# A two-layer decoder trunk on one core: the first layer reordered, and the dense feed-forward fed before its row norm is known

## What is computed

```python
x = x + concat([s5_mixer(u), memory_attention(q, mem)]) @ l0_w_out
h = rms_norm(x, ffn_norm)                      # y = x * rsqrt(mean(x*x) + eps) * g
x = x + (silu(h @ w_gate) * (h @ w_up)) @ w_down
...
kv = shared_kv(x);  x = x + concat([moba_attention(..), memory_attention(..)]) @ l1_w_out
h = rms_norm(x, l1_ffn_norm)
x = x + moe_swiglu(h, router, w_gate, w_up, w_down)     # top 2 of 8 experts
```

## Time and profile before

| | us |
|---|---|
| three runs | 1522.99, 1524.78, 1525.23 (median 1524.78) |
| the profiled execution | 1524.49 |
| its span | 1522.8 |
| PE busy | 1471.9 (97%) |
| DVE busy | 1190.7 (78%) |
| ACT busy | 973.8 (64%) |
| experts start (first expert matmul) | 520.2 |

### The profile page before, as it was taken

One profiled execution on the slowest core, in us unless ns is written; L12 is line 12 of the kernel. 1 busy time (PEld: TensorE's weight loads), 2 busy tenths in 40 slices (PEclk: granted clock), 3 DMA queues, 4 the chain that ended last, 5 costly groups with the idle time before them and its releaser, 6 DMA issues.

```text
span 1522.8 us, 20929 instructions
## 1 busy us (share of the span) xinstructions
PE 1471.9 (97%) x7935; PEld 1237.2 (81%) x7935; DVE 1190.7 (78%) x1211; ACT 973.8 (64%) x947; POOL 128.2 (8%) x151
## 2 busy tenths in 40 slices
PE   7999999999978999999999999999999999999997
PEld 3788789999756988888888888888888888888886
DVE  6883545455684798898898889889889889888987
ACT  4324354444451777777787787787777778778775
POOL 1751300000544000000000000000000000000000
PEclk9999999999999999999999999999999999999998
DMA  8434655344342499999999999999999999999992
GB/s 240 124 48 178 237 201 180 139 139 138 111 166 98 178 356 366 342 358 365 371 332 365 371 335 356 375 338 357 364 341 359 365 371 330 366 372 334 355 376 92
DMA packets 193090, 425.97 MB, mean 280 GB/s; under 512 B 14002, under 2 KB 23088, under 8 KB 192944
## 3 DMA queue, kind: packets, MB, share of 16 engines
q1 hardware_dynamic: 192736, 425.23, 78.2%
q10 hardware_dynamic: 304, 0.06, 0.0%
HBM read 421.67 MB, written 1.05 MB: 278 GB/s over the span
## 4 chain that ended last, share of the span: by engine, by line
PE 89%; DVE 5%; ACT 4%; issue 1%; POOL 1%; ACTq 0%; DVEq 0%
PE bank L413 75%; PE bank L513 3%; PE bank L433 2%; PE bank L466 2%; PE bank L849 2%; PE bank L861 1%; DVE w_lo L1733 1%; ACT work L1321 1%; PE bank L656 1%; DVE work L1726 1%; PE bank L567 1%; ACT work L1203 1%; DVE w_lo L1886 0%; PE bank L549 0%; PE bank L680 0%
## 5 line engine op out<-in xcount | busy, mean ns | idle before, releaser
L1886 DVE TENSOR_TENSOR w_lo<-ring,w_hi 128x2048 fp32r<-128x2048 f32 x342 | 779.9, 2289 | 104.6 <-ACT w_hi L1469 104.0
L1469 ACT ACTIVATE w_hi<-ring 128x2048 fp32r<-128x2048 f32 x342 | 651.9, 1918 | 125.5 <-PE bank L413 124.6
L413 PE MATMUL bank<-w_hi,xg_hl 128*128 128x512 f32 x1792 | 557.1, 392 | 0.2 <-issue 0.2
L413 PEld LDWEIGHTS bank<-w_hi,xg_hl 128*128 128x128 f32 x1792 | 332.8, 188 | 67.5 <-issue 0.4
L413 PE MATMUL bank<-w_lo,xg_hl 128*128 128x512 f32 x896 | 349.4, 390 | 0.0
L413 PE MATMUL bank<-w_hi,at_hl 128*128 128x512 f32 x896 | 277.5, 391 | 0.0
L413 PEld LDWEIGHTS bank<-w_lo,xg_hl 128*128 128x128 f32 x896 | 168.2, 188 | 35.8
L413 PEld LDWEIGHTS bank<-w_hi,at_hl 128*128 128x128 f32 x896 | 167.0, 188 | 34.0
L413 PE MATMUL bank<-w_lo,at_hl 128*128 128x512 f32 x448 | 174.5, 389 | 0.0
L1783 DVE TENSOR_TENSOR fpart_hl<-ring,fpart_hl 128x1024 fp32r<-128x1024 f32 x66 | 80.7, 1225 | 90.8 <-ACT fpart_hl L1384 90.4
L1384 ACT ACTIVATE fpart_hl<-ring 128x1024 fp32r<-128x1024 f32 x66 | 69.7, 1059 | 98.2 <-PE bank L413 98.2
(11 more groups left out here) (235 smaller groups left out, 1213.4 us busy)
## 6 DMA issues: line engine op xcount, KB each, us to landing
ring<-in_l_moe_w_gate SPq DMA_DIRECT2D x58, 2048.0 KB, 7.8
ring<-in_l_moe_w_up SPq DMA_DIRECT2D x57, 2048.0 KB, 7.8
ring<-in_l_moe_w_down SPq DMA_DIRECT2D x56, 2048.0 KB, 7.8
ring<-in_l_ffn_w_gate SPq DMA_DIRECT2D x5, 2048.0 KB, 8.8
ring<-in_l_ffn_w_up SPq DMA_DIRECT2D x5, 2048.0 KB, 8.9
ring<-in_l_ffn_w_down SPq DMA_DIRECT2D x5, 2048.0 KB, 7.7
ring<-in_l_w_in SPq DMA_DIRECT2D x4, 2048.0 KB, 8.4
ring<-in_l_w_out SPq DMA_DIRECT2D x4, 2048.0 KB, 8.1
```

The lines of the kernel that those rows point to most:

```text
L413: last = mm(p, lhsT=xs[a], rhs=ws[b], start=start and q == 0, stop=stop and q == 2, **kw)
L1469: ac(w_hi(n), at(e_slot(q) * SLOT + j * HALF, HALF), ACT.Copy).then_inc(S("hi"), 1)
L1886: tt(LO[e_slot(q)][:, j * HALF:(j + 1) * HALF], at(e_slot(q) * SLOT + j * HALF, HALF), w_hi(n).bitcast(fp), ALU.subtract).then_inc(S("lo"), 1)
```

## The change

The tensor block has most of it; line numbers of the new kernel are some 4 to 50 higher.

- First layer. `idle_products(5, 12)` stands ahead of `win0a`. The coefficient transposes are no longer together between the two halves of `win0b` but 16 ahead of k = 0 and 16 ahead of k = 5 of the second half. The three `Ug` flips are spread among the twelve `Bm` flips, `V` waits for each pair of `Bm` blocks when it comes to them rather than for all twelve, and `memkv1` no longer waits for the copies of `q0T` and `mkT`.
- wout0. The low halves get a buffer of their own (`CTL0`). `wide` takes both row halves m in one loop over k for `wout0a`; `wout0b` runs m = 0, then the flips of the first four column blocks of XS, then m = 1.
- Dense feed-forward. XS is flipped without the norm's row scale (`rows_f0` is gone, and the two `idle_products` with it). The last four blocks are flipped ahead of part 1. ACT squares after the flips are read. The scale comes back in two places: DVE makes two diagonal matrices `DG`, PE multiplies them by ones (`rsb`, ahead of part 4), DVE copies that to `RSB` and multiplies every gate block by it (`gate`) before the Silu; the residual of the down product is scaled by row (`scalar_tensor_tensor`).
- kv: the last down part finishes both row halves of columns 0 to 511 first, the flips follow block by block, `proj_kv` waits for each pair of blocks, and ACT squares after its first two blocks.
- wout1 and router: `wout1a` with both halves in one loop, flips after `wout1b`'s first half and at its end, router inputs in their own buffer `HTF`, idle products of 3, 5 and 8 calls where 6, 7 and 25 were.

```diff
+            idle_products(5, 12)
             proj_half("win0a", HT, "win0", 0, (0, 1, 2, 3), "xT0")
...
-            proj_half("win0b", HT, "win0", 1, (0, 1, 2, 3), None, coefficients)
+            proj_half("win0b", HT, "win0", 1, (0, 1, 2, 3), None, {0: (6, cm, "cm"), 5: (7, pw, "pw")})
...
-            for n in range(12):
-                read_out(pe, ("Bm", n))
             for n in range(3):
                 read_out(pe, ("Ug", n))
             vb = [unit(pe, ("V", n), n) for n in range(3)]
             for j in range(PAIRS):
+                if j % 4 == 0:
+                    for ri in range(2):
+                        read_out(pe, ("Bm", 6 * ri + j // 4))
...
-            for h, name in enumerate(("wout0a", "wout0b")):
-                for m in range(TM):
-                    wide(name, "wout0", h, m, 2 * h + m, (CTH0, HTHL[:, 1]), "wout0", state_space_and_memory)
+            def flip_cols(tag, q, b, parts):
+
+                p = unit(pe, ("T" + tag, q), b)
                 for m in range(TM):
+                    read_out(pe, parts[m])
+                    for k in (2 * q, 2 * q + 1):
+                        last = transpose(p[:, (k % 2) * T + m * P:(k % 2) * T + (m + 1) * P], XS[:, m, k * P:(k + 1) * P])
+                ready(last, ("T" + tag, q))
+
+            wide("wout0a", "wout0", 0, (0, 1), (0, 1), (CTH0, CTL0), "wout0", state_space_and_memory)
             mem_keys(1, (6, 7))
+            wide("wout0b", "wout0", 1, (0,), (4,), (CTH0, CTL0), "wout0")
+            for q in range(2):
+                flip_cols("f0", q, 6 + q, [("wout0", 0, m) for m in range(TM)])
+            wide("wout0b", "wout0", 1, (1,), (5,), (CTH0, CTL0), "wout0")
...
-            idle_products(5, 24)
-            rows_to_cols("f0")
-            idle_products(5, 7)
-            for q in range(4):
-                read_out(pe, ("Tf0", q))
...
+                if n == 1:
+                    for q in range(2, 4):
+                        flip_cols("f0", q, 4 + q, [("wout0", 1, m) for m in range(TM)])
+                if n == 4:
+                    pe.wait_ge(S("ones_f"), 1)
+                    pe.wait_ge(S("dg"), 1)
+                    p = unit(pe, "rsb", 6)
+                    for m in range(TM):
+                        last = mm(p[:, m * P:(m + 1) * P], lhsT=ONESF, rhs=DG[:, m], start=(m == 0), stop=True, skip_group_check=True)
+                    ready(last, "rsb")
...
-            rows_to_cols("kv", XS, [("ffn", b) for b in range(4)])
-            pe.wait_ge(S("ct_kv_act"), 2)
-            pe.wait_ge(S("ct_kv_dve"), 2)
-            proj_kv("kv", CT, "kv", (4, 5))
+            for q in range(4):
+                flip_cols("kv", q, q, [("ffn", q // 2 * 2 + m) for m in range(TM)])
+            proj_kv("kv", CT, "kv", (4, 5), lambda k: pe.wait_ge(S("ct_kv_act" if k < 4 else "ct_kv_dve"), k % 4 // 2 + 1))
...
+            idle_products(2, 5)
             pe.wait_ge(S("ld_router"), 16)
...
-            idle_products(7, 25)
+            idle_products(2, 8)
             pe.wait_ge(S("sel"), 1)
...
@@ scalar
-            norm("f0", 0, [("wout0", h, m) for h in range(2) for m in range(TM)])
+            mem_keys_out(1)
             for q in range(4):
                 p = got(act, ("Tf0", q))
...
+            for h in range(2):
+                for m in range(TM):
+                    read_out(act, ("wout0", h, m))
+            for m in range(TM):
+                ac(JUNK0[:, m], XS[:, m], ACT.Square, accum_out=ss[:, m:m + 1]).then_inc(S("ss_f0"), 1)
...
@@ vector
+                if n == NFP + 1:
+                    dve.wait_ge(S("rs_f0"), 1)
+                    for m in range(TM):
+                        last = tsc(DG[:, m], ident, rs[:, m:m + 1], None, ALU.mult)
+                    last.then_inc(S("dg"), 1)
...
+                    def gate(f):
+                        p = got(dve, ("h", c, f))
+                        tt(SG0[:, f], p[:, 0:T], RSB, ALU.mult).then_inc(S("gs"), 1)
+
+                    gate(0)
                     for f in range(FCH[c] // P):
+                        if f + 1 < FCH[c] // P:
+                            gate(f + 1)
                         n_sg += 1
                         dve.wait_ge(S("sg0"), n_sg)
                         free(tt(HID0[:, f], SG0[:, f], PS[units[("h", c, f)][0]][:, T:2 * T], ALU.mult), ("h", c, f))
```

191 lines of the change are left out of this document (107 added, 84 removed).

## The result

The changed kernel took 1513.19 us in the median (1512.1 to 1514.56, 4 runs) against 1525.01 for the kernel before (1522.99 to 1525.34, 4 runs): a ratio of 0.9929, 95% interval 0.9917 to 0.9942. The forecast was 1509.3, with a range of 1502.5 to 1515.0; faster was right, and 11.8 us were gained of the 15.2 forecast. The profiled execution took 1513.77, its span is 1512.0.

A forecast was written before the change was run, and what follows sets the result against it. The prediction took PE, busy for 97% of the span, as the bound, with only gaps and clock to win: -5.0 - 9.4 - 2.9 + 2.1 = -15.2 against 1524.49 gave 1509.3 us, range 1502.5 to 1515.0.

The forecast's parts named there:

- hand-off: From wout0 into the feed-forward: -1.2 us in wout0 and -11.7 off the gap before the first feed-forward matmul.
- stage A: The first layer up to Y: -5.0 us, bounds -1.5 and -5.9.
- I assume that it goes, since the idle time is shorter: In wout0: the half-speed stretch behind the second wait disappears, giving back 1.6 us.
- What comes back (+3.5): Feed-forward costs: flips before part 1 +1.0, lead running out by part 3 +0.9, rsb +0.5, gate at u0 +1.1.
- The gate at u0: First feed-forward chunk: four more PSUM reads on DVE add 1.43 us, exposed less Silu overlap: +1.1.
- rival 4: Feed-forward: DVE becomes the bound, taking back all 15.2 us from 1.4 us per gate; 1536 at 1.9; chance 0.02.
- Stage C: kv, from the last down part to kv's first matmul: -2.9 us, bounds -2 to -3.3.
- Stage D: wout1 to the experts: -0.6 + 2.7 = +2.1 us, bounds -0.6 to +3.6.
- The rule on the clock: Throttled is the default and activity releases it; by this alone Stage D would lose 2 to 4 us.
- I get 3.4 for the CA chain: First layer, POOL: the CA chain moves 3.4 us earlier, ends at 80.5, and K begins there.
- only become idle time: First layer before Y: the 1.7 us memkv1 saves turn into waiting for the Tm DMAs, without gain.
- Rival 1: Start filler runs cold, ends near 15.8 and delays the projection: stage A only -2.1, time 1512.2; chance 0.17.

The follow-up runs named there:

- again: The changed kernel itself, unedited, timed and profiled a second time: 1511.51 us, ratio 0.9920 to the kernel before.
- gate2: The changed kernel with every gate multiplication done twice, the first into unused space: 1515.79 us, ratio 0.9940 to the kernel before.
- three: The changed kernel with filler calls in three waits: 11 ahead of Y, 12 ahead of g1, 22 between router and placement: 1509.2 us, ratio 0.9903.
- y11: The changed kernel with 11 filler calls added between memkv1 and Y: 1512.55 us, ratio 0.9928 to the kernel before.
- router27: The changed kernel with 27 filler calls between router and placement in place of 8: 1510.91 us, ratio 0.9919 to the kernel before.
- win1ord: The changed kernel with ACT's two kv norm squares moved behind the high halves of win1a: 1512.67 us, ratio 0.9928 to the kernel before.
- undoA: The changed kernel with most of its first-layer part undone; memkv1 still skips the waits for q0T and mkT: 1514.25 us, ratio 0.9944.
- lateflips: The changed kernel with the first four column blocks' flips moved from the middle of wout0b to its end: 1513.71 us, ratio 0.9926.
- tm2q: The changed kernel with half of the 16 Tm transfers issued from ACT's queue instead of SP's: 1511.62 us, ratio 0.9930.
- start7: The changed kernel with 7 filler calls ahead of the first projection in place of 12: 1512.2 us, ratio 0.9925.

## Why the prediction was right, and where it was not

The total fell into the range because the hand-off and kv, most of the forecast's gain, came nearly as worked out. It missed the forecast's own time by 3.9 us; in the profile the first layer came 4.8 short. The prediction named a gain of less than 3 us in stage A as a sign that it is wrong, and that sign came: to the yT flips the gain is 0.2 in the changed kernel's profile, and of the six profiles with the same code only "again" has more than 3.

**The hand-off (11.7 off the gap): right.** Measured -11.47 up to the first FFN matmul, where the parts -1.2 and -11.7 made -12.9. The missing 1.4 is the half-speed stretch in wout0. The waits came as forecast (0.62 and 1.97 for 0.5 and 2.1), but the step "I assume that it goes, since the idle time is shorter" holds only at times: in three of thirteen profiles the stretch went and the part was -13.1, in the others it stayed. That is no matter of the 1.97 us, which were the same in both cases.

**What comes back (+3.5): +2.5.** The flips before part 1 took 0.8 and rsb 0.4; the wait of 0.9 before part 3 never came, so the three parts of lead were enough even with ACT's two squares in front. The gate at u0 cost 1.25 (2.87 against 1.62) for a forecast of 1.1. In gate2 four more of them added 1.08 us there and no wait elsewhere, so rival 4's mechanism is far off. What the sum put at nothing is the clock behind that longer wait: 1.3 to 2.9 us in five of eleven profiles, nothing in the first one.

**Stage C (-2.9): -3.5** for the whole stretch from g1 to kv, in the profiles with no slow clock behind g1. The flips of the right half follow without any wait.

**Stage D (+2.1): +1.9, and partly by luck.** Idle 4.63 us for some 6, placement 2.30 for 2.3, the filler behind it as slow as forecast, the gather not slow: 2.0 lost where 2.7 were forecast. Up to placement the first profile gained next to nothing, since 1.2 us went to wout1's slow start, which the forecast did not have; in "again", without it, the stage is +0.7. The rule on the clock that was cited beside the sum, "TensorE: Matmul & The Clock Gate" of the Trainium skill, "What's actually happening", agrees in its direction: with nothing but filler, three has 9.6 us from placement to the experts and the changed kernel 11.6.

**Stage A (-5.0): two steps failed.** On PE alone the terms were about right. In the five profiles with fast filler the first projection ended 2.5 to 2.8 us earlier, for 2.4 forecast, and in the five with slow filler 1.0 to 1.2; the second half gave 1.4 for 1.7.

The first step that failed is "I get 3.4 for the CA chain". It rests on a wait inside the chain, for DVE's copies of u, that was to shrink because these come earlier. It did not shrink (2.74 us in the first profile, 2.41 before): the chain is as long as before in every profile (38.0 to 38.2 us), and DVE came to its copies only after its own W products, at 60.97 and before at 61.99. So the chain moved as far as its start, by 1.0 in the first profile, 2.0 in "again" and 2.5 to 2.8 in y11, router27, win1ord and three. K followed: 83.03 in the first profile, 81.2 to 82.0 where the filler was fast, 80.5 forecast. In "again", which no slow stretch disturbed, this is all that is missing: K and the yT flips are 3.5 earlier, not 5.0.

The second is the sentence that the time which memkv1 saves will "only become idle time", put at nothing. PE now waits up to 2.1 us ahead of K and 1.9 to 2.6 ahead of Y, and behind such waits it ran at 1.2 GHz for some microseconds in most profiles: 1.7 us at Y in four of eight, and more around the Bm flips, V and K in some. In the first profile K is 2.5 earlier, the Tm transfers and what stands before them took 0.65 longer and Y 1.7, and 0.2 is left. In total time the part is worth 2 to 4 us by undoA, not settled beyond the intervals and without memkv1's share.

Rival 1 had its number nearer, and in the first profile its picture to the tenth (filler to 15.84, 15.8 forecast), and that picture came in five profiles of ten; a chance of 0.17 was too low for it. It is not the whole: it explains 1.7 us in those profiles and nothing in "again".

**Not forecast:** +0.6 from kv to wout1, which is not settled: win1b waits 1.7 us in "again", lateflips and tm2q too, and there the stretch is 77.8, 1.0 less than before. And -0.6 in the expert loop, of which nothing shows a cause.

## What to carry to other kernels

Take a norm's scale out of a product's input and multiply it into the small result: what leaves the path is the whole chain of squares, root, scaling and flips, and the price is one multiplication where the first result is waited for. Time won ahead of a bound that does not move becomes idle time of the matmul engine, and that can have a price of its own behind it. Before you count on a chain on another engine to move, look whether its own work or the wait inside it sets its length. Fill a wait only where its length is the same in every run and to its end: at placement 36 records that left 2.4 us gave back 0.8 of the 2.0 us, 44 that fitted all of it, and 54 delayed placement by 1.1. One profile per kernel is too little to size an edit of a few microseconds where the clock takes part.

## What the runs showed of the hardware

- After the same idle time PE ran at 1.2 GHz in some executions and not in others: Y's 96 records took 7.10 us in the changed kernel, router27, start7 and gate2, and 5.43 in lateflips, win1ord, undoA and "again", after waits of 1.87 to 2.64 us; 1.87, 1.96, 1.99 and 2.10 were followed by full speed, 1.95 by half. Behind the 1.97 us in wout0 the clock stayed at 1.00 in three profiles and fell in the others. The changed kernel itself had spans from 1506.1 to 1512.8 us.
- At the start of the program the granted clock reads 1.00 while records take the times of half speed: 24 filler records in 5.03 us, and undoA's projection 16.20 with 1.00 over 14.1 to 18.0. Only the earlier trace rows had 0.50 there. At the start the records' own durations are the better witness.
- Filler that begins at half speed stays there for long: 16 records took 3.4 to 3.8 us, 44 took 8.05 and 54 took 9.20 (0.18 and 0.17 each in the mean, 0.115 at full speed).
- In tm2q each issue took longer when two queues issued at once: 1.3 to 1.4 us each, where one queue alone took 0.8.
